# Loading attention's keys and values during the Fourier stage, and splitting the keys once over all 128 partitions

## The reference

```python
x = layer_norm(x, ln_emb_g, ln_emb_b)
proj = x @ w_in                      # 1280 columns: u 512, q 512, k 128, v 128
heads = concat([fourier_mix(u, w_fourier),                  # FNet part, 4 groups of 128 channels
                windowed_attention(q, k, v, sink_logits)])  # 8 query heads, 2 key/value heads of 64
x = layer_norm(ALPHA * x + heads @ w_out, ...)
h = square(relu(x @ w_ff1))
x = layer_norm(ALPHA * x + h @ w_ff2, ...)

# windowed_attention, for a block of 128 queries and its 3 blocks of keys
scores = q @ k.T / sqrt(64) - slope * distance       # masked outside +-128 tokens
m = max(max(scores), sink);  p = exp(scores - m)
out = (p / (sum(p) + exp(sink - m))) @ v
```

## Time and profile before

| what | value |
|---|---|
| median of three runs | 2599.19 us |
| the profiled execution | 2601.09 us, of which the span of the trace is 2599.4 us |
| TensorE busy (matmul) | 2402.2 us, 92% of the span |
| VectorE busy | 1603.8 us, 62% |
| ScalarE busy | 1099.0 us, 42% |
| GpSimd busy | 179.2 us, 7% |
| DMA | 543.10 MB, mean 209 GB/s |
| granted TensorE clock, mean | 0.966 of full |

### The profile page before, as it was taken

One profiled execution on the slowest core, in us unless ns is written; L12 is line 12 of the kernel. 1 busy time (PEld: TensorE's weight loads), 2 busy tenths in 40 slices (PEclk: granted clock), 3 DMA queues, 4 the chain that ended last, 5 costly groups with the idle time before them and its releaser, 6 DMA issues. The chain is left out here.

```text
span 2599.4 us, 35337 instructions
## 1 busy us (share of the span) xinstructions
PE 2402.2 (92%) x12192; PEld 2099.0 (81%) x12192; DVE 1603.8 (62%) x2225; ACT 1099.0 (42%) x1745; POOL 179.2 (7%) x246
## 2 busy tenths in 40 slices
PE   4999969499879996999989998997999999999997
PEld 3888859499868874888889998997888888888885
DVE  7544156566556666666666666664546577669666
ACT  2111132588721114444465555554433344444442
POOL 1000000121112220000000000000000000001001
PEclk9999979699989997999999999998999999999998
DMA  7675242532255666555576676675876659877973
GB/s 271 255 262 232 112 147 81 147 75 71 57 192 187 239 255 227 198 213 210 209 280 231 248 267 248 224 251 185 274 258 194 195 173 323 254 226 243 304 226 113
DMA packets 217768, 543.10 MB, mean 209 GB/s; under 512 B 21376, under 2 KB 89984, under 8 KB 198208
## 3 DMA queue, kind: packets, MB, share of 16 engines
q1 hardware_dynamic: 200352, 476.99, 52.7%
q0 software_dynamic: 17312, 64.76, 8.0%
HBM read 361.31 MB, written 180.36 MB: 208 GB/s over the span
## 5 line engine op out<-in xcount | busy, mean ns | idle before, releaser
L1791 DVE TENSOR_TENSOR e_lo<-e_raw,e_hi 128x896 fp32r<-128x896 f32 (+1 forms) x336 | 379.1, 1135 | 266.7 <-ACT e_hi L1774 258.9
L1774 ACT CAST e_hi<-e_raw 128x896 fp32r<-128x896 f32 (+1 forms) x336 | 330.4, 983 | 428.1 <-PE e_bank L65 387.5
L63 PE MATMUL e_bank<-e_hi,e_lo 128*128 128x512 f32 x1120 | 436.9, 390 | 15.9 <-DVE e_lo L1791 15.9
L64 PE MATMUL e_bank<-e_lo,e_hi 128*128 128x512 f32 x1120 | 436.6, 390 | 0.0
L65 PE MATMUL e_bank<-e_hi 128*128 128x512 f32 x1120 | 436.6, 390 | 0.0
L63 PE MATMUL u_bank<-u_x_hi,u_wa_lo 128*128 128x384 f32 (+1 forms) x768 | 275.1, 358 | 39.0 <-DVE u_x_first L1428 22.3
L65 PE MATMUL u_bank<-u_x_hi,u_wa_hi 128*128 128x384 f32 (+1 forms) x768 | 273.7, 356 | 0.0
L63 PEld LDWEIGHTS e_bank<-e_hi,e_lo 128*128 128x128 f32 x1120 | 210.9, 188 | 60.2 <-DVE e_lo L1791 16.2
L64 PEld LDWEIGHTS e_bank<-e_lo,e_hi 128*128 128x128 f32 x1120 | 210.9, 188 | 43.9
L65 PEld LDWEIGHTS e_bank<-e_hi 128*128 128x128 f32 x1120 | 210.8, 188 | 43.8
L63 PE MATMUL u_bank<-u_x_hi,u_wb_lo 128*128 128x384 f32 (+1 forms) x576 | 203.4, 353 | 4.5 <-DVE u_c L1499 3.0
(11 more groups left out here) (194 smaller groups left out, 4347.7 us busy)
## 6 DMA issues: line engine op xcount, KB each, us to landing
u_w_raw<-w_ff SPq DMA_DIRECT2D x48, 1024.0 KB, 7.7
e_raw<-s_t SPq DMA_DIRECT2D x192, 256.0 KB, 3.8
e_raw<-s_h SPq DMA_DIRECT2D x224, 192.0 KB, 2.8
e_raw<-w_ff SPq DMA_DIRECT2D x144, 256.0 KB, 3.8
u_w_sum<-s_ws SPq DMA_DIRECT2D x32, 1024.0 KB, 4.8
e_raw<-s_h SPq DMA_DIRECT2D x112, 256.0 KB, 2.7
s_h<-u_h_sum SPq DMA_DIRECT2D x32, 768.0 KB, 6.9
s_h<-u_h SPq DMA_DIRECT2D x96, 192.0 KB, 2.3
```

Source lines behind the costliest of these rows:

```text
L63: tensor.matmul(out, w_lo, m_hi, start=first, stop=False, skip_group_check=again)
L64: tensor.matmul(out, w_hi, m_lo, start=False, stop=False, skip_group_check=again)
L1774: act.copy(part(hi, n), part(raw, n)).then_inc(hi_done, 1)
L1791: dve.tensor_tensor(part(lo, n), part(raw, n), part(hi, n).bitcast(F32), ALU.subtract).then_inc(split, 1)
```

## The change

- The identity tile is made once in `build` and loaded once, in `embed_project`. Attention's own load of it goes, with TensorE's wait for it.
- The sink logits are loaded by `load_mixing` in the first stage.
- `c_vt_raw` (10 KB in each partition) is made in `build`; `wf` and `chan` of the Fourier stage are now views of its first columns. `c_k_raw` (20 KB) is made before the Fourier stage, whose raw tables (`t_raw`) are now a view of it.
- The ten key loads and the value load are issued by SyncE in the Fourier stage, after the store of unit 1, behind waits for `ab_split` 2 (the last reader of `wf` and `chan` is done) and for all five tables split.
- In `attend`, ScalarE rounds each group of keys once, into `c_ka`, and VectorE makes the rest once over 128 partitions, into `c_kb`. `c_ka` is now the high part in both halves and `c_kb` the low part. The two matmuls of a score are the same, and their sum is too.

```diff
@@ fourier, SyncE, in the loop over units @@
                              ).then_inc(out_st[n % 2], 16)
+                if n == 1:
+                    sp.wait_ge(ab_split, 2)
+                    sp.wait_ge(t_split, len(tiles))
+                    load_keys_values(sp)
@@ attend, SyncE @@
-            for g in range(NG):
-                tok = slice(g * GRP, (g + 1) * GRP)
-                for half in range(2):
-                    sp.dma_start(k_raw[half * HD:(half + 1) * HD, :, tok],
-                                 proj_d[KROW:KROW + P, tok].rearrange("(v d) t -> d v t", d=HD)
-                                 ).then_inc(k_ld[g], 16)
-                if g == 0:
-                    sp.dma_start(snk[:], sink.partition_broadcast(P)).then_inc(const_in, 16)
-                    sp.dma_start(ident[:], ident_d).then_inc(const_in, 16)
-                    sp.dma_start(vt_raw[:], proj_d[VROW:, :]).then_inc(v_ld, 16)
             sp.dma_start(bias[:], bias_d).then_inc(bias_in, 16)
@@ attend, VectorE @@
-            dve.wait_ge(const_in, 32)
+            dve.wait_ge(snk_in, 16)
             dve.tensor_scalar(neg_sink[:], snk[:], -1.0, None, ALU.mult)
             for g in range(NG):
                 tok = slice(g * GRP, (g + 1) * GRP)
-                dve.wait_ge(k_rounded, 2 * g + 2)
-                dve.tensor_tensor(kb[0:HD, :, tok], k_raw[0:HD, :, tok], kb[0:HD, :, tok].bitcast(F32),
-                                  ALU.subtract).then_inc(k_split, 1)
-                dve.tensor_tensor(ka[HD:P, :, tok], k_raw[HD:P, :, tok], ka[HD:P, :, tok].bitcast(F32),
-                                  ALU.subtract).then_inc(k_split, 1)
+                dve.wait_ge(k_rounded, g + 1)
+                dve.tensor_tensor(kb[:, :, tok], k_raw[:, :, tok], ka[:, :, tok].bitcast(F32), ALU.subtract
+                                  ).then_inc(k_split, 1)
@@ attend, ScalarE @@
                 act.copy(ka[:, :, tok], k_raw[:, :, tok]).then_inc(k_rounded, 1)
-                act.copy(kb[:, :, tok], k_raw[:, :, tok]).then_inc(k_rounded, 1)
@@ attend, TensorE @@
-            pe.wait_ge(const_in, 32)
             pe.wait_ge(v_ld, 16)
...
-            pe.wait_ge(k_split, 2 * NG)
+            pe.wait_ge(k_split, NG)
@@ build @@
+        vt_raw = ctx.enter_context(nc.sbuf_tensor("c_vt_raw", [P, TOK], F32))
+        wf = vt_raw[:, 0:NFG * P].rearrange("p (g d) -> p g d", d=P)
+        chan = vt_raw[:, NFG * P:(NFG + 2) * P].rearrange("p (i d) -> p i d", d=P)
...
+            sp.dma_start(snk[:], d["sink"].partition_broadcast(P)).then_inc(snk_in, 16)
...
+        k_raw = ctx.enter_context(nc.sbuf_tensor("c_k_raw", [P, NKV, TOK], F32))
+
+        def load_keys_values(sp):
+            for g in range(NG):
+                tok = slice(g * GRP, (g + 1) * GRP)
+                for half in range(2):
+                    sp.dma_start(k_raw[half * HD:(half + 1) * HD, :, tok],
+                                 s["proj"][KROW:KROW + P, tok].rearrange("(v d) t -> d v t", d=HD)
+                                 ).then_inc(k_ld[g], 16)
+            sp.dma_start(vt_raw[:], s["proj"][VROW:, :]).then_inc(v_ld, 16)
```

More of the change, by code:

```diff
@@ L93, in sems, with embed_project @@
         return [self.sem(f"{name}{i}") for i in range(n)]
-def embed_project(nc, x, ln_g, ln_b, w_in, ident_d, xn_d, proj_d, w2_d, t_d, load_mixing):
+def embed_project(nc, x, ln_g, ln_b, w_in, ident, ident_d, xn_d, proj_d, w2_d, t_d, load_mixing):
     WR = 4
@@ L101, in embed_project @@
         al = Phase(nc, ctx, "a")
-        ident = al.sb("ident", [P, P])
         gain = al.sb("gain", [P, D])
@@ L329, in _, with fourier @@
                     mm.then_inc(proj_done, 1)
-def fourier(nc, proj_d, mixing, table_ds, heads_d):
+def fourier(nc, proj_d, mixing, k_raw, table_ds, heads_d, load_keys_values):
     QMAX = max(n for _, n in SEQS) // 4
@@ L346, in fourier @@
         ab_lo = al.sb("ab_lo", [P, 2, FOUR], F32R)
-        t_raw = al.sb("t_raw", [P, 2, WIDE])
+        t_raw = k_raw[:].rearrange("p v t -> p (v t)")[:, 0:2 * WIDE].rearrange("p (s w) -> p s w", s=2)
         t0_hi = al.sb("t0_hi", [P, 1, FOUR + 2], F32R)
@@ L673, in _ @@
             for i in range(2):
-                pe.matmul(bank[:, 6 + i, :], chan[:, i, :], wf[:].rearrange("p g d -> p (g d)"), start=True, stop=True
+                pe.matmul(bank[:, 6 + i, :], chan[:, i, :], wf.rearrange("p g d -> p (g d)"), start=True, stop=True
                           ).then_inc(ab_done, 1)
@@ L686, in _, with attend @@
                     channels(n + 1, 1)
-def attend(nc, proj_d, sink, bias_d, ident_d, heads_d):
+def attend(nc, proj_d, bias_d, ident, operands, heads_d):
     AHEAD = {"scores": 6, "bias": 5, "exp": 4, "turn": 3, "high": 2, "rest": 1, "values": 0}
@@ L705, in attend @@
         al = Phase(nc, ctx, "c")
-        ident = al.sb("ident", [P, P])
+        k_raw, vt_raw, snk, k_ld, v_ld, snk_in = operands
         bias = al.sb("bias", [P, NH, 3 * P])
         neg_sink = al.sb("neg_sink", [P, NH])
-        snk = al.sb("snk", [P, NH])
-        k_raw = al.sb("k_raw", [P, NKV, TOK])
         ka = al.sb("ka", [P, NKV, TOK], F32R)
         kb = al.sb("kb", [P, NKV, TOK], F32R)
-        vt_raw = al.sb("vt_raw", [P, TOK])
         v_rows = al.sb("v_rows", [P, NB, NKV, HD])
@@ L729, in attend @@
         pv = al.ps("pv", [P, 2, NH, HD])
-        const_in, bias_in = al.sem("const_in"), al.sem("bias_in")
-        k_ld, k_rounded, k_split = al.sems("k_ld", NG), al.sem("k_rounded"), al.sem("k_split")
-        v_ld, v_turned = al.sem("v_ld"), al.sem("v_turned")
+        bias_in = al.sem("bias_in")
+        k_rounded, k_split = al.sem("k_rounded"), al.sem("k_split")
+        v_turned = al.sem("v_turned")
         v_done = al.sem("v_done")
@@ L1899, in build @@
     with ExitStack() as ctx:
-        chan = ctx.enter_context(nc.sbuf_tensor("b_chan", [P, 2, P], F32))
-        wf = ctx.enter_context(nc.sbuf_tensor("b_wf", [P, NFG, P], F32))
-        in_ld = nc.alloc_semaphore("b_in_ld")
+        ident = ctx.enter_context(nc.sbuf_tensor("ac_ident", [P, P], F32))
+        snk = ctx.enter_context(nc.sbuf_tensor("c_snk", [P, NH], F32))
+        vt_raw = ctx.enter_context(nc.sbuf_tensor("c_vt_raw", [P, TOK], F32))
+        wf = vt_raw[:, 0:NFG * P].rearrange("p (g d) -> p g d", d=P)
@@ L1905, in load_mixing @@
+        chan = vt_raw[:, NFG * P:(NFG + 2) * P].rearrange("p (i d) -> p i d", d=P)
+        in_ld, snk_in, v_ld = (nc.alloc_semaphore(name) for name in ("b_in_ld", "c_snk_in", "c_v_ld"))
+        k_ld = [nc.alloc_semaphore(f"c_k_ld{g}") for g in range(NG)]
         def load_mixing(sp):
-            sp.dma_start(wf[:], d["w_fourier"].rearrange("g c d -> c g d")).then_inc(in_ld, 16)
-            sp.dma_start(chan[:], d["chan"]).then_inc(in_ld, 16)
-        embed_project(nc, d["x"], d["ln_emb_g"], d["ln_emb_b"], d["w_in"], d["ident"], s["x_norm"], s["proj"],
+            sp.dma_start(wf, d["w_fourier"].rearrange("g c d -> c g d")).then_inc(in_ld, 16)
+            sp.dma_start(chan, d["chan"]).then_inc(in_ld, 16)
+            sp.dma_start(snk[:], d["sink"].partition_broadcast(P)).then_inc(snk_in, 16)
@@ L1909, in build @@
+        embed_project(nc, d["x"], d["ln_emb_g"], d["ln_emb_b"], d["w_in"], ident, d["ident"], s["x_norm"], s["proj"],
                       d["w_ff2"], s["t"], load_mixing)
-        fourier(nc, s["proj"], (chan, wf, in_ld), [d["table0"], d["table1"]], s["heads"])
-    attend(nc, s["proj"], d["sink"], d["bias"], d["ident"], s["heads"])
+        k_raw = ctx.enter_context(nc.sbuf_tensor("c_k_raw", [P, NKV, TOK], F32))
[7 more added lines that the diff above has]
+            sp.dma_start(vt_raw[:], s["proj"][VROW:, :]).then_inc(v_ld, 16)
@@ L1912, in build @@
+        fourier(nc, s["proj"], (chan, wf, in_ld), k_raw, [d["table0"], d["table1"]], s["heads"], load_keys_values)
+        attend(nc, s["proj"], d["bias"], ident, (k_raw, vt_raw, snk, k_ld, v_ld, snk_in), s["heads"])
     with ExitStack() as ctx:
```

## The result

The changed kernel takes 2581.18 us (median of four runs, 2579.41 to 2581.82) against 2599.84 for the kernel before in the same measurement. The ratio is 0.9923, with a 95% interval of 0.9912 to 0.9935: 18.7 us faster. Forecast were 2579.1 us and a gain of 20.1. The span of the profiled execution fell from 2599.4 to 2579.1 us, by 20.3. A second measurement of both on another occasion gave 2581.33 against 2600.37, ratio 0.9929 (0.9915 to 0.9942).

The account below looks back on a forecast made before the run. Attention's start was taken as bound by loads, with TensorE waiting. First score from 493.36 to 473.3 gains 20.1 us, all other terms 0: 2599.19 - 20.1 = 2579.1 us for the median, range 2575 to 2586.

Parts of the forecast that it names:

- What bounds: Attention's start: 31.4 us of getting ready, set by loads; the keys last by a little, the distance table next.
- The table: Attention's start: distance table on SyncE's queue, last to be ready, at 471.9 by even shares, then rest_q and first score 473.3.
- The queries: Attention's start: first pair on GpSimd's queue lands at 469.4 if both queues share evenly, rounded by 470.5.
- served in order of issue: Fallback for attention's start: table lands at 468.1, queries are last, first score near 472.
- The half for the keys: Attention's start: one rounding and one subtraction less per key group; with ten of each, keys end at 475.9, last by 4 us.
- The rule against the change: Attention's start: GpSimd's first rounding meets VectorE's last subtraction, starting up to 1.2 us later; the sum stays.
- The loads in the Fourier stage: Fourier stage: key and value loads landed by 434, delaying neither waits nor unit 2's store; cover 12 us, cost 0.
- The clock: TensorE's granted clock, low at the first score, rising some 7 us after it; taken as 0, 2 us kept in range.
- A: Rival, attention's start: table or queries come late, table landing between 476 and 481; gain 11 to 16 us; chance 0.11.
- B: Rival, attention's start: more gained, with TensorE at high clock for first scores and an early table; 2575 us; chance 0.06.
- C: Rival, Fourier stage: slower, the 3.93 MB of loads block unit 2's store; 2607 us worked out; chance 0.02.
- D: Rival, attention's start: something other than these loads holds it, first score near 490; 2596 to 2599 us; chance 0.03.

## Why the prediction was right, point by point

*What bounds.* Right. Keys a little ahead of the table were last before. With the key work halved and the loads left in place, `rest_q` waited 1.17 us for the table and the first score came 1.9 us earlier, as the 1.8 us between the two had said. But "loads set this" was only part of it for the keys: in the kernel before the last eight subtractions follow one another without a gap from 481.85 on, and with one for each group the keys are split 2.9 us sooner behind the start (26.5 for 29.4).

*The keys.* 469.7 forecast, 469.05 measured: 5.77 us for five. The step took the duration of 128 partitions from another operation of the same shape. It held: one subtraction takes 1.22 us over 64 partitions and 1.23 over 128.

*The values.* 470.0 forecast, 468.38 + 1.09 = 469.5 measured.

*The table.* 471.9 forecast, 470.0 measured. *The queries.* Landed at 469.4 and rounded at 470.5 forecast; 472.1 and 473.2 measured. This is the step that was mis-sized, in the words of the prediction "if the two queues share evenly". They do not. SyncE's queue moved 1.28 of the table's 1.57 MB from 463 to 467, and only then did the queries' packets begin. The bytes were right, their order wrong. So the queries were last and not the table, 1.3 us behind the forecast for the first score (474.65 for 473.3). That the total came out so near is in part luck: both operands were misplaced, the table by 1.9 and the queries by 2.7 us, and the one that came last in their stead was only 1.3 us off. My fallback "served in order of issue" had the right order and a first score "near 472", 2.7 us too early. It moved the queries at the table's 416 GB/s, where from 469 to 472 they passed alone at some 210 GB/s, and it took the first pair to be through before the second began. Measured, 0.94 of the 1.05 MB of both pairs had passed between 467 and 472.1, when the first pair was there.

The Trainium skill, "DMA: Bandwidth & Descriptors", section "Queues, rings and completion order", has each DMA engine take its queues in turn, a packet at a time. The run with the loads last agrees once both queues are moving, with 72 packets of each from 479 to 483. But the prediction's condition "packets alike in length" does not hold there: the table's are 12 KB (0.88 MB over 72) and the queries' under 4 (0.26 MB over 72), so turns that are even in packets give the table three times the bytes. And the turns do not begin with the issue. The queries' first packet came 4.5 us after their issue in the kernel after and 6.1 us with the loads last, but 2.0 us in the kernel before and 1.4 us with the table held back. The size of the packets alone does not decide it: the 4.5 us were behind packets of 12 KB, the 6.1 us behind packets of 2 KB, and in the kernel before the same 2 KB packets let the queries in. How much SyncE's queue already holds when GpSimd's is filled differs between these runs and could be the reason; that was not tested.

*The half for the keys "carries about 4 of the 20 us".* It was 5.05 up to the first score; in the run with only the loads moved the ten subtractions end at 477.9 instead of 475.9. The forecast lacked the 1.5 us by which the two GpSimd roundings stretch them, and 0.6 us for the second rounding before the first of them.

*The rule against the change.* The meeting that was priced did not take place: in the changed kernel GpSimd's first rounding came after the keys. Its second one met `rest_q` and took 1.17 us instead of 1.04, which held up nothing. Where the first ones met, the rule held, and the later instruction grew by 0.3 to 1.0 us. Its price up to the first score was 0.84 us with the queries early (6.61 for 5.77) and 1.5 us with only the loads moved; the prediction had set about 1.

*The loads in the Fourier stage: 0.* Right. SyncE was free at 423.6 (422 forecast), the loads were landed by 435.0 (434), and the store of unit 2 was issued on time. VectorE's waits in the stage are as before, and its last operation ends at 457.4 instead of 457.1, but the store of unit 0, ahead of the loads, is already 0.25 us later.

*The clock.* I took it for 0 and kept 2 us. It was low at the first score, as forecast, and rose 5.4 us after it instead of 6.9. It is at 0.50 from 476 to 479 and at 1.00 from 480 to 482. In both profiles of the changed kernel the stretch from the first score to mix_out is shorter than before, by 0.9 and 1.3 us, which the earlier rise may explain; it was not tested by itself. The mix_out stage was 0.8 us shorter in the first profile and 1.6 longer in the second, so that part is not the change's. This is 705 to 725 us of the first profile, with the granted clock in the third column from the end:

```profile
705.00:725.00 20.00, 15.59 (x54) 11.99 (x55) 11.30 (x11) 8.31 (x9) 0.89 (x1) 0.82 0.56 206
```

And the same stretch of the second profile:

```profile
705.00:725.00 20.00, 17.14 (x50) 12.82 (x49) 8.90 (x9) 5.91 (x7) 0.00 (x0) 0.69 0.49 183
```

At 0.82 four more matmuls were done in the stretch than at 0.69, in less busy time, though mix_out had started 1.6 us later. So of the 20.3 us in the first pair of profiles 18.7 are the way to the first score, and the remaining 1.6 are within what two profiles of one kernel differ by in a single stage. The 18.7 are also the gain by the medians.

*The rivals.* A (late table or queries) in a small form: the queries were 2.7 us late and the table was not; its price was 4 to 9 us. B, C and D did not occur.

## What to carry to other kernels

When a stage starts cold, write down for every operand when it is issued, when it lands, and what work follows it before the first matmul; the gain of an early load is the distance from the last of these to the next, and here the next four stood within 4.2 us (keys 469.05, values 469.5, table 470.0, queries 473.2). A large transfer issued just ahead of a small one that is needed sooner can take the place of the wait that was removed, as the table did here. Moving it behind the small one gained nothing, for then it was missed itself; moving it ahead of the stage gained about 3 us. Look at what an operation will stand beside after the change; of two engines that never met before, one may then wait for the other.

## What the runs showed of the hardware that I had not expected

- In the kernel after there are 3.5 us in which one DMA queue moved 1.07 MB in 12 KB packets and the other, issued half a microsecond later, none. With the first queue empty the other's queries were ready 5.6 us after issue instead of 9.5. Yet with the loads last, the same two kinds of packets took turns one for one (72 and 72 in 4 us).
- A VectorE subtraction with two SBUF inputs and a GpSimd rounding did not run at the same time. The later of the two grew by the overlap less 0.14 us: subtractions of 1.22 us became up to 2.06, roundings of 1.04 us up to 2.08. The earlier one kept its length.
- The same kernel's mix_out stage took 268.2 us in one profile and 270.6 in another, with a granted clock of 0.82 and 0.69 from 705 to 725 us.
